# The second MLP product of a one-core transformer layer as seven half-size products

## The reference, cut to what matters

```
hn = rms_norm(h, norm_mlp)               # (512, 1024)
a = relu(hn @ w_mlp_in)                  # (512, 1024) @ (1024, 4096)
h = h + (a * a) @ w_mlp_out              # (512, 4096) @ (4096, 1024)
return rms_norm(h, norm_final)
```

## Time and profile before

| | |
|---|---|
| median of 3 runs | 984.47 us (984.45 to 987.2) |
| the profiled execution, its own time | 984.29 us |
| its span, first to last instruction | 982.6 us |
| mean granted TensorE clock | 0.997 of full speed |
| busy: TensorE, VectorE, ScalarE, GpSimd | 955.0, 478.7, 349.4, 14.1 us |
| the MLP's matmuls, from 622 us on | 352 us of the span |

### The profile page before, as it was taken

How to read it: one execution, slowest core, us unless ns; L and a number is a source line. 1 busy time by engine, 2 the same in 40 slices (tenths; PEclk the granted TensorE clock), 3 DMA queues, 4 the chain that set the end, 5 groups by cost and what they waited for, 6 DMA issues and landing times.

```text
span 982.6 us, 11650 instructions
## 1 busy us (share of the span) xinstructions
PE 955.0 (97%) x4677; PEld 775.6 (79%) x4677; DVE 478.7 (49%) x873; ACT 349.4 (36%) x562; POOL 14.1 (1%) x38
## 2 busy tenths in 40 slices
PE   7999999999998999999999999999999999999996
PEld 6778777777776788889877768888888888888885
...
GB/s 282 91 51 74 87 86 44 44 86 86 86 1 86 65 235 86 107 129 138 141 86 86 86 86 86 86 86 85 86 88 123 125 94 86 85 86 86 91 39 85
DMA packets 44205, 92.60 MB, mean 94 GB/s; under 512 B 1676, under 2 KB 1768, under 8 KB 44152
## 3 DMA queue, kind: packets, MB, share of 16 engines
...
HBM read 89.76 MB, written 2.10 MB: 93 GB/s over the span
## 4 chain that ended last, share of the span: by engine, by line
PE 87%; DVE 8%; ACT 3%; issue 1%; DMA 1%; SPq 0%; ACTq 0%; DVEq 0%
PE bank L1067 76%; DVE w_lo L797 2%; PE bank L1240 1%; PE bank L1191 1%; DVE conv_acc L817 1%; PE bank L1080 1%; PE bank L1134 1%; ACT w_hi L588 1%; PE bank L1178 1%; DMA stage<-in_w_in 1%; PE bank L1161 1%; PE bank L1146 1%; PE bank L1218 1%; PE bank L1205 1%; ACT prob_t L588 0%
## 5 line engine op out<-in xcount | busy, mean ns | idle before, releaser
L1067 PE MATMUL bank<-act_hi,w_hi 128*128 128x512 f32 (+2 forms) x624 | 245.5, 393 | 2.4 <-DVE act_lo L893 2.4
L1067 PE MATMUL bank<-act_hi,w_lo 128*128 128x512 f32 (+2 forms) x624 | 240.6, 386 | 0.0
L1067 PE MATMUL bank<-act_lo,w_hi 128*128 128x512 f32 (+2 forms) x624 | 240.3, 385 | 0.0
L797 DVE TENSOR_TENSOR w_lo<-stage,w_hi 128x1024 fp32r<-128x1024 f32 x156 | 184.0, 1221 | 109.8 <-ACT w_hi L588 109.7
L588 ACT ACTIVATE w_hi<-stage 128x1024 fp32r<-128x1024 f32 x156 | 156.4, 1052 | 175.4 <-PE bank L1067 169.7
L1067 PE MATMUL bank<-w_hi,act_hi 128*128 128x512 f32 x448 | 176.8, 395 | 5.0 <-DVE act_lo L893 3.4
L1067 PE MATMUL bank<-w_lo,act_hi 128*128 128x512 f32 x448 | 175.1, 391 | 0.0
L1067 PE MATMUL bank<-w_hi,act_lo 128*128 128x512 f32 x448 | 175.1, 391 | 0.0
L1067 PEld LDWEIGHTS bank<-act_hi,w_hi 128*128 128x128 f32 x624 | 117.4, 188 | 24.6 <-issue 2.6
L1067 PEld LDWEIGHTS bank<-act_hi,w_lo 128*128 128x128 f32 x624 | 117.2, 188 | 23.7
L1067 PEld LDWEIGHTS bank<-act_lo,w_hi 128*128 128x128 f32 x624 | 117.4, 188 | 21.8
...
## 6 DMA issues: line engine op xcount, KB each, us to landing
stage<-in_w_in SPq DMA_DIRECT2D x22, 1024.0 KB, 5.0
stage<-in_w_mlp_in SPq DMA_DIRECT2D x16, 1024.0 KB, 5.2
stage<-in_w_mlp_out SPq DMA_DIRECT2D x16, 1024.0 KB, 5.1
stage<-in_w_xkv SPq DMA_DIRECT2D x8, 1024.0 KB, 5.0
stage<-in_w_mix_out SPq DMA_DIRECT2D x4, 1024.0 KB, 5.1
stage<-in_w_xq SPq DMA_DIRECT2D x4, 1024.0 KB, 5.1
stage<-in_w_xo SPq DMA_DIRECT2D x4, 1024.0 KB, 5.0
...
```

What stands on the lines that cost most here:

```text
L797: dve.tensor_tensor(w_lo[:, r:r + 2, :], src, w_hi[:, r:r + 2, :].bitcast(F32), ALU.subtract)\
L1067: ins = pe.matmul(dst, still[q], moving[q], start=(k == 0 and q == 0), stop=(k == nk - 1 and q == 2))
```

## The change

The second product of a round is a 512 x 1024 matrix of activations times a 1024 x 1024 block of weights. It is seen as 2 x 2 blocks: A11, A12 (first half of the tokens; even and odd 128-column tiles of hidden units), A21, A22 (second half of the tokens), and B11, B12, B21, B22 (even and odd row slabs; output columns 0 to 511 and 512 to 1023). It is computed by seven products of half size in each dimension, in a Strassen-Winograd scheme:

- Sums of weights on GpSimd, in place in the staging buffers (`weight_sum`): B12 - B11 (second product), B22 - B12 (sixth), B22 - (B12 - B11) (third) and B21 - that (seventh); each as two instructions of 128x1024. The third waits until the pairs of the second product are split, since it writes over them.
- Sums of activations on VectorE (`act_sums`), in place in `ff`, four of 128x256 for each pair of tiles, with three more high and low parts.
- ReLU and the square are both done by ScalarE, in `ff`.
- `product` on TensorE: for each of the seven products two halves of 12 matmuls (128 tokens each), written to one of three pairs of PSUM banks. A half uses the same form of matmul as `mlp_out` before. A round has 14 pairs of weight slabs in this product instead of 8.
- `fold` on VectorE: after each half, PSUM is added to one of seven places: four scratch tensors `p1`, `p5`, `p6`, `p7` and three quarters of `h_tok`. In the last round, ScalarE copies the first two products, and the sixth is added twice.
- `combine` on VectorE: 13 sums of 128x1024 that bring the scratch tensors together in `h_tok`: 8 in the last round's `mlp_in` units, 5 after the third, fourth and fifth products of the last round. The final norms come after the fifth product's halves (tokens 0 to 255) and the seventh's (256 to 511).
- There are three staging buffers for MLP weights. B22 and B21 share one: B21 is loaded when the fourth product's weights (B22) are split.

Core of the diff:

```diff
-STAGES = 2
+STAGES = 3
 
 WARM_UP = 20
+
+
+PRODUCTS = 7
+PRODUCT = ((0, 0), (1, 0), (2, 0), (4, 2), (5, 3), (3, 1), (6, 0))
+SUMMED = {1: (1, 0), 5: (2, 1), 2: (2, 0), 6: (3, 0)}
...
-            (f"mlp_out{2 * r}", "w_mlp_out", r * DM, KT, 0, NT),
-            (f"mlp_out{2 * r + 1}", "w_mlp_out", r * DM, KT, HALF_W, NT),
+            (f"mlp_out{r}", "w_mlp_out", r * DM, 4 * PRODUCTS, 0, 2),
...
+def make_lots():
+
+    lots, of_pair, freed, sum_no = [], {}, {}, {}
+    buf, sums, turn = 1, 0, 1
+    for n, (name, w, row0, nk, col0, _) in enumerate(UNITS):
+        n_buf = STAGES if name.startswith("mlp") else 2
+        pair = SLAB0[n] // 2
+        if in_products(n):
+            a, b, c = ((buf + turn * (1 + i)) % n_buf for i in range(3))
+            first = len(lots)
+            for (h, half), buf in zip(((0, 0), (0, 1), (1, 1), (1, 0)), (a, b, c, c)):
+                lots.append((n, h, half, buf))
+            for q in range(PRODUCTS):
+                for e in range(2):
+                    of_pair[pair + 2 * q + e] = (first + PRODUCT[q][1], e, q)
+            for q in SUMMED:
+                for e in range(2):
+                    sums += 1
+                    sum_no[pair + 2 * q + e] = sums
+            freed[first] = ("low", pair + 14)
+            freed[first + 1] = ("low", pair + 12)
+            freed[first + 2] = ("low", pair + 8)
+            freed[first + 3] = ("sum", sum_no[pair + 13])
+            turn = -turn
+            buf = c - turn
...
+    for t in range(8):
+        after(FIRST_HALF[n - 2] + 2 + t, ("combine", t))
+    for t, (m, q) in enumerate(((1, 2), (1, 2), (0, 3), (0, 4), (1, 4))):
+        after(HALF_AT[(n, m, q)], ("combine", 8 + t))
     for i in range(NT):
-        after(group_end(n, i) - 1, ("norm", 3 * NT + 2 + i))
+        after(HALF_AT[(n, i % 2, 4 if i < 2 else 6)], ("norm", 3 * NT + 2 + i))
+    for v in range(FF // P // 2):
+        n, j = UNIT[f"mlp_in{v // 2}"], 2 * (v % 2) + 1
+        after(group_end(n, j) - 1 + (1 if v % 4 < 3 else 0), ("act_sums", v))
...
+        if in_products(n):
+            steps.append(("fold", i))
+            steps += [("split_weights", p) for p in pairs.get(i, [])] + a
+            continue
...
+                if buf in held:
+                    what, count = FREED[held[buf]]
+                    if what == "sum":
+                        sp.wait_ge(s_wsum, count)
+                        count = SLAB0[LOTS[held[buf]][0]] // 2 + 10
+                    sp.wait_ge(s_low, count)
+                held[buf] = lot
+                sp.dma_start(stage[buf][:], src).then_inc(s_lot[buf], 16)
...
+            def weight_sum(pair):
+
+                lot, e, q = LOT_OF[pair]
+                plus, minus = (lot - PRODUCT[q][1] + i for i in SUMMED[q])
+                rows = slice(2 * e, 2 * e + 2)
+                first = pair - e - 2 * q
+                lot_landed(pool, plus)
+                if q in (1, 5):
+                    lot_landed(pool, minus)
+                if q != 5:
+                    pool.wait_ge(s_low, {1: first, 2: first + 2, 6: first + 4}[q] + e + 1)
+                if q == 6:
+                    pool.wait_ge(s_wsum, SUM_NO[pair - 8])
+                elif q != 1:
+                    pool.wait_ge(s_wsum, SUM_NO[first + 2 + e])
+                dst = stage[LOTS[lot][3]][:, rows, :]
+                pool.tensor_tensor(dst, stage[LOTS[plus][3]][:, rows, :], stage[LOTS[minus][3]][:, rows, :],
+                                   ALU.subtract).then_inc(s_wsum, 1)
...
-                    if a >= 2:
-                        act.wait_ge(s_relu2, a - 1)
-                    act.activation(relu[:, a % 2, :], b[:], ACT.Relu).then_inc(free, 1)
+                    t = a % KT
+                    act.activation(ff[:, t, :], b[:], ACT.Relu).then_inc(free, 1)
+                    taken(act, g)
+                    act.activation(ff[:, t, :], ff[:, t, :], ACT.Square).then_inc(s_relu2, 1)
                     act.wait_ge(s_relu2, a + 1)
-                    copy(act2_hi[:, a % KT, :], relu2[:, a % 2, :]).then_inc(s_ah, 1)
...
+            def fold(i):
+
+                n, m, q, *_ = HALVES[i]
+                r = order(n)
+                src = two[1 + (PRODUCTS * r + q) % 3][:, m, :]
+                if r == last_r and q < 2:
+                    return
+                dst = (p1, p5, p6, quarter(0, 1), quarter(0, 0), p7, quarter(1, 0))[q][:, m, :]
+                if r == last_r and q in (2, 5):
+                    if q == 2:
+                        dve.wait_ge(s_kept, m + 1)
+                    dve.wait_ge(s_half, i + 1)
+                    if q == 2:
+                        dve.tensor_tensor(dst, src, p1[:, m, :], ALU.add).then_inc(s_fold, 1)
+                    else:
+                        for h in (quarter(1, 1), quarter(1, 0)):
+                            dve.tensor_tensor(h[:, m, :], src, h[:, m, :], ALU.add).then_inc(s_fold, 1)
+                    return
+                if r > 0:
+                    folded(dve, r - 1, q, m)
+                elif q in (3, 4, 6):
+                    taken(dve, GROUP0[UNIT[f"x_out{int(q == 3)}"]] + (2 + m if q == 6 else m))
+                if r == last_r and q == 6:
+                    folded(dve, r, 5, m)
+                dve.wait_ge(s_half, i + 1)
+                if r == 0 and q in (0, 1, 2, 5):
+                    dve.tensor_copy(dst, src).then_inc(s_fold, 1)
+                else:
+                    dve.tensor_tensor(dst, src, dst, ALU.add).then_inc(s_fold, 1)
+
+            def combine(t):
+
+                dst, more = ((quarter(0, 0), p1), (p6[:], p1), (quarter(0, 1), p6), (quarter(0, 1), p5), (p7[:], p6),
+                             (quarter(1, 1), p7), (quarter(1, 0), p7), (quarter(1, 1), p5),
+                             (p5[:], p6), (quarter(0, 1), p5), (quarter(0, 0), p1), (quarter(1, 1), p5),
+                             (quarter(1, 0), p6))[t]
+                if t == 0:
+                    folded(dve, last_r - 1, 6, 1)
+                elif t >= 8:
+                    if t == 8:
+                        dve.wait_ge(s_kept, 4)
+                    folded(dve, last_r, *((2, 1), (2, 1), (3, 0), (4, 0), (4, 1))[t - 8])
+                dve.wait_ge(s_combined, t)
+                dve.tensor_tensor(dst, dst, more[:], ALU.add).then_inc(s_combined, 1)
+                dve.wait_ge(s_combined, t + 1)
...
+            def act_sums(v):
+
+                u, half = v % 4, TOK // 2
+                a11, a21 = ff[:, 2 * u, 0:half], ff[:, 2 * u, half:TOK]
+                a12, a22 = ff[:, 2 * u + 1, 0:half], ff[:, 2 * u + 1, half:TOK]
+                dve.wait_ge(s_al, 2 * v + 2)
+                dve.tensor_tensor(a22, a21, a22, ALU.add).then_inc(s_asum, 1)
+                dve.tensor_tensor(a21, a11, a21, ALU.subtract)
+                dve.wait_ge(s_asum, 3 * v + 1)
+                dve.tensor_tensor(a11, a22, a11, ALU.subtract).then_inc(s_asum, 1)
+                dve.wait_ge(s_asum, 3 * v + 2)
+                dve.tensor_tensor(a12, a12, a11, ALU.subtract).then_inc(s_asum, 1)
...
+                n, m, q, *_ = HALVES[i]
+                r, what = order(n), PRODUCT[q][0]
+                dst = two[1 + (PRODUCTS * r + q) % 3][:, m, :]
+                low, high = (slice(h + P * m, h + P * m + P) for h in (0, TOK // 2))
+                if q >= 3:
+                    folded(pe, r, q - 3, m)
+                elif r > 0:
+                    folded(pe, r - 1, q - 3 + PRODUCTS, m)
+                for u in range(4):
+                    v = 4 * r + u
+                    slab = SLAB0[n] + 4 * q + u
+                    if m == 0:
+                        if u % 2 == 0:
+                            pe.wait_ge(s_low, slab // 2 + 1)
+                        if what in (0, 5, 6):
+                            pe.wait_ge(s_al, 2 * v + (1 if what == 0 else 2))
+                        else:
+                            pe.wait_ge(s_sl, 3 * v + (0, 1, 2, 2, 3)[what])
+                    hi, lo = ((act2_hi[:, 2 * u, low], act2_lo[:, 2 * u, low]),
...
+                    for g, (s, w) in enumerate(((hi, w_hi), (hi, w_lo), (lo, w_hi))):
+                        ins = pe.matmul(dst, s, w[:, slab % RING, :], start=(u == 0 and g == 0),
+                                        stop=(u == 3 and g == 2))
+                ins.then_inc(s_half, 1)
```

218 lines of the change are left out of this document (149 added, 69 removed).

## The result

The changed kernel takes **1012.93 us** (median of 4 runs, 1010.55 to 1014.98) against 984.46 us of the kernel before on the same chip: a ratio of 1.027, 95% interval 1.0247 to 1.0294. It is 2.7% slower (the two medians alone give 1.029). The forecast was 988, range 974 to 994: the likeliest sign was right, the size was not.

The account below looks back on a forecast made before the run. TensorE, busy 97% of the span, was taken as the bound: 984.3 - 21.8 (matmuls) + 11.8 (tail) + 1.0 (instruction waits) + 13.0 (GpSimd sums holding VectorE) = 988.3, say 988 us; range 974 to 994.

Parts of the forecast that it names:

- The saved matmuls, -21.8: Second MLP product on TensorE: 96 fewer matmuls at 0.2268 us each, a full gain of 21.8 us.
- The tail, +11.8: Last round: VectorE's queue falls behind, so 17.1 us instead of 5.3 pass after TensorE's end; bounds 7 and 13.
- The 1.0 us for waits of one instruction on the one before it: VectorE's queue in the last round: about 30 waits of 0.035 us each, adding 1.0 us.
- the case of the hold: GpSimd sums block VectorE's two-SBUF-input instructions for a whole sum: 988 us, 984.4 to 992.7, chance 0.48.
- the sign "some 22 us": End of kernel: the last scaling would end some 22 us behind TensorE's end if the forecast was right.
- The case of no hold, 975.3: Rival: GpSimd's sums are hidden altogether and TensorE never waits in the MLP; 975.3 us, chance 0.28.
- The slack: Fifth product of each round: B21's first weights ready 1.4 us before TensorE wants them, the tightest place.
- Elsewhere: First 620 us keep their order but for two pairs of weights: 0, bounds -1 and +1 us.
- Its size, +13.0: VectorE held by GpSimd sums: 7.6 us of TensorE waits in three rounds plus 5.4 in the last.
- the sums ahead of the second product: GpSimd's sums there were taken to hide on an idle engine, at no cost.
- the third product's sums at u = 0.75: First of two GpSimd sums runs to 2.85, making the last tile's rest 0.85 us late; second sum adds 2.1.
- rival 3: Fifth product: both seventh-product sums run before VectorE's first B21 pair, another 2.1 us a round; 996.7 us, chance 0.09.

Follow-up runs that it names:

- Experiment 1: Changed kernel with each GpSimd weight sum cut from 1024 to 16 columns, all waits and places kept: 978.97 us, ratio 0.9916 to the kernel before.
- Experiment 7: Experiment 1 without the last five combining sums: 974.79 us.
- experiment 8: Against the kernel before: seven products in the first three rounds only, last round as before, weight sums on VectorE: 970.77 us, ratio 0.9837.
- experiment 6: Kernel before plus 32 unused GpSimd sums, placed where VectorE has adds out of PSUM or nothing to do: 992.58 us (before 986.09).
- experiment 4: Kernel before plus 32 GpSimd sums of 128x1024 on a separate tensor nothing reads, near the change's places: 1008.25 us, ratio 1.0218.
- Experiments 3: Changed kernel with only the seventh product's two GpSimd sums made later, after the second pair of B21's weights: 1007.51 us, ratio 1.022.
- 10: Changed kernel with the third product's sums on VectorE and the seventh's made late, the other four on GpSimd: 1002.66 us.

## Right and wrong, by the steps of the prediction

**The saved matmuls, -21.8: right.** Experiment 1 has 21.4 of them.

**The tail, +11.8: right**, 8.9 to 20.7 us. Experiment 7 shows it to be VectorE's queue, experiment 8 that it goes with the last round's combining. Five sums are worth 5.4 of it, where 6.1 were counted. The 1.0 us for waits of one instruction on the one before it, meant on top, does not show: the tail is 11.8 longer with them in it. In the case of the hold, another 5.4 us were put behind TensorE's end in the last round (the sign "some 22 us"). They are not there: the last scaling ends 17.2 us behind it, as without a hold, since TensorE itself was late, with 8.1 us of waits in that round.

**The case of no hold, 975.3: right as a sum.** Experiment 1 is that case, at 0.9916 x 984.5 = 976.2; its profiled execution took 979.0, which is 984.3 - 21.4 + 11.4 and 4.7 for a later start of the MLP. The slack is right too: the first rest of the activation sums was put at u = 5.0 and ends at 4.8 there; B21 was put at 12.9 when sent for and is at 12.1, and its landing takes 5.5 us rather than 5.1. Its first pair is ready 1.8 us early in round 2. (By the prediction's own times, 20.3 against 21.8, the slack is 1.5, not 1.4.)

**"Elsewhere", 0 with bounds of -1 and +1: too small.** It measured +3.2, of which 1.2 is the wait at 340 us for the two pairs of weights that the prediction named and put at nothing.

**That there is a hold: right. Its size, +13.0: wrong, and this is the step that failed.** It measured 27.9 us of waits and 7.1 of slower steps. Four things were missing from it, all seen in round 2. The rows are the timeline of the changed kernel, 748 to 773 us (start, duration); its first product starts at 762.50, which is u = 0:

```profile
748.07 11.18 POOL L707 TENSOR_TENSOR stage<-stage,stage 128x1024 f32<-128x1024 f32 x4 [45.32 <-DVE w_lo L947]
...
754.50 2.50 DVE L1005 TENSOR_TENSOR ff<-ff 128x256 f32<-128x256 f32 x1
756.92 2.61 DVE L1006 TENSOR_TENSOR ff<-ff 128x256 f32<-128x256 f32 x1
757.03 0.42 ACT L720 ACTIVATE act_hi<-ff 128x256 fp32r<-128x256 f32 x1 [3.29 <-DVE ff L1005]
...
764.25 0.57 ACT L781 ACTIVATE ff<-bank 128x512 f32<-128x512 f32 x1
764.78 6.04 POOL L707 TENSOR_TENSOR stage<-stage,stage 128x1024 f32<-128x1024 f32 x2 [5.54 <-DVE w_lo L947]
766.18 2.40 DVE L1072 TENSOR_TENSOR act_lo<-ff,act_hi 128x512 fp32r<-128x512 f32 x1 [0.40 <-ACT act_hi L720]
768.62 2.48 DVE L1005 TENSOR_TENSOR ff<-ff 128x256 f32<-128x256 f32 x1
771.03 0.41 DVE L1006 TENSOR_TENSOR ff<-ff 128x256 f32<-128x256 f32 x1
772.15 0.42 DVE L1012 TENSOR_TENSOR ff_lo<-ff,act_hi 128x256 fp32r<-128x256 f32 x1
```

1. *I let the sums ahead of the second product hide.* The second and sixth product's four sums run for 11.18 us in the stage of the first MLP product and hold the rests and sums of the third pair of activation tiles. ScalarE's queue is in order too: its copy of that pair waits 3.29 us for L1005, and behind it stand the second product's weight copies and the last tile's ReLU. That ReLU starts at 764.25, u = 1.75; with small sums it starts at u = 0.2. ScalarE's own instructions kept their length; it was late because it stood behind the held engine. In the last round these sums also meet a combining sum (3.41 us instead of 1.22) and, behind it, the rest that the first product needs (2.77 instead of 0.69): its wait of 2.84 us.
2. *I started the third product's sums at u = 0.75, and did not carry their delay to the second product.* By the prediction's own figures the rest that TensorE needs there at 7.5 would have been ready at 5.0 + 2.95 = 7.95, so the sum lacked a wait of 0.4 us a round. The two sums start at u = 2.3, and hold the last tile's rest (2.40 instead of 0.69) and the first of the four activation sums (2.48 instead of 0.42), 3.8 us together. The rest that TensorE needs ends at 772.57, u = 10.07, against 7.5: the wait of 2.65 us. The 1.5 us of the late ReLU and the 3.8 are the 5.3 that lie between this rest and that of experiment 1 (u = 4.8).
3. *I took VectorE's two rests as one piece that GpSimd cannot enter.* It can: at 786.70 the pair from B21 took 5.75 instead of 2.36, because the second sum came in between them. The prediction had this as rival 3, at 0.09, and spoke against it from a row in which GpSimd did nothing. No row of the kernel before could tell, and the chance should have been even.
4. *I priced a sum at 2.1 us.* It takes 2.39 alone (experiment 6) and 2.92 on average in the changed kernel. The upper bound, both inputs in turn at VectorE's rate, 2.44, was the right one for it alone; the 2.25 that the prediction gave beside its own price is also under what was measured. The longest sum in the changed kernel takes 3.38: a sum above 3 us had been set down as a sign that the forecast was wrong altogether, and so had a wait at a product other than the fifth.

And one thing belongs to no instruction: **a wait of TensorE can cost more than itself.** After the last round's wait of 2.84 us at 945 us, seven matmuls have a pitch of 0.43 us. Windows of TensorE (stretch, us, busy, PEclk, DMA share, GB/s) and two rows within:

```profile
936.00:945.00 9.00, 6.42 (x29) 1.00 0.00 0
945.90:949.40 3.50, 3.50 (x10) 0.52 0.02 5
...
946.24 0.63 PE L1317 MATMUL bank<-w_lo,act_hi 128*128 128x512 f32 x1
946.66 0.63 PE L1317 MATMUL bank<-w_hi,act_lo 128*128 128x512 f32 x1
```

A granted clock of 0.52 is the 1.2 GHz level; at 1.00 it is 2.4. Steps of this pitch cost 3.0 us here and 6.8 in experiment 4. They follow some of the waits and not others of the same length (none follows the 2.65 us at the second product of the first three rounds), so I can say what they cost, not when they come.

**The rivals.** The likeliest case was the right mechanism, and the third rival was a part of the truth; their sum at the third's price, 996.7, is still 16 us short. Of the 1012.7 measured, 984.3 - 21.8 + 11.8 + 27.9 + 7.1 + 3.2 is 1012.5. What would have held the time is a range that let the hold reach every SBUF instruction of VectorE that meets a sum: 8 sums of 2.4 us a round are 19 us of possible hold, and TensorE lost 6.5 to 8.1 of them in waits.

**What stays open.** Why the half clock follows one wait and not another; what the longer steps that are neither waits nor at half clock come from; and whether the sums on GpSimd can be placed so that they meet only adds out of PSUM. Experiments 3, 6 and 10 moved them, and each time they met something; for the changed kernel no placement without a hold was found.
